# Branch A's attention scores as three products of rounded halves in place of one fp32 product, with another order of steps

## The reference, cut to what matters

```python
for layer in range(DEPTH):                      # DEPTH = 2
    u = rms_norm(h, norm_pre[layer])
    proj = u @ w_in[layer]                      # split into the columns of A, B, C, D
    y_a = mla_branch(...) * silu(a_g)
    y_b, y_c, y_d = ...                         # dilated, top-k sparse, differential attention
    y = concatenate([y_a, y_b, y_c, y_d]) @ w_out[layer]
    h = h + rms_norm(y, norm_post[layer])

# in mla_branch, for each block of 128 queries:
    s = (einsum('bqhd,bshd->bhqs', qn, k_nope) + einsum('bqhd,bsd->bhqs', qr, k_rope)) * scale
    s = where(keys <= t, s, NEG_INF)
    p = softmax(s);  out = einsum('bhqs,bshd->bqhd', p, v)
```

## Time and profile before

| | before |
|---|---|
| median of 3 runs | 665.01 us |
| lowest, highest | 664.68, 666.29 us |
| the profiled execution | 664.22 us, span 662.4 us |
| PE busy | 636.5 us, 96% of the span |
| DVE, ACT, POOL busy | 392.7, 355.8, 241.4 us (59%, 54%, 36%) |
| mean granted TensorE clock | 0.993 |

### The profile page before, as it was taken

The page is one execution under the profiler, slowest core; times in us unless marked ns, Lnnn a source line. Parts: engine busy times, 40 slices in busy tenths (PEclk is TensorE's granted clock), DMA queues, the critical chain, the costliest instruction groups (busy, mean ns, idle before and its releaser), DMA issues. The chain is left out here.

```text
span 662.4 us, 10348 instructions
## 1 busy us (share of the span) xinstructions
PE 636.5 (96%) x3700; PEld 521.5 (79%) x3700; DVE 392.7 (59%) x986; ACT 355.8 (54%) x818; POOL 241.4 (36%) x209
## 2 busy tenths in 40 slices
PE   6999999999999999999999999999999999999996
PEld 4977887777778767679998897777777876776996
DVE  4322775986868558640381249679787765764124
ACT  4522734585465586862353454456655648678121
POOL 1443343345043781023416433343424359300330
PEclk9999999998999999999999999999999999999999
DMA  8447967553452403212372587644535222130202
GB/s 261 127 138 227 269 206 230 194 160 89 97 140 72 139 1 116 76 28 101 98 223 64 171 261 228 173 137 118 169 84 128 77 82 79 64 128 1 96 33 96
DMA packets 78589, 85.78 MB, mean 129 GB/s; under 512 B 21013, under 2 KB 62229, under 8 KB 78537
## 3 DMA queue, kind: packets, MB, share of 16 engines
q1 hardware_dynamic: 78537, 85.11, 42.9%
HBM read 70.38 MB, written 13.94 MB: 127 GB/s over the span
## 5 line engine op out<-in xcount | busy, mean ns | idle before, releaser
L727 POOL TENSOR_TENSOR w_low<-w_raw,w_high 128x512 fp32r<-128x512 f32 (+2 forms) x156 | 198.9, 1306 | 346.2 <-ACT w_high L769 346.1
L1343 PE MATMUL bank<-uT,w_high 128*128 128x512 f32 x400 | 160.4, 401 | 1.7 <-DVE cqlow L1145 0.9
L1345 PE MATMUL bank<-uT,w_low 128*128 128x512 f32 x400 | 158.6, 397 | 0.0
L1344 PE MATMUL bank<-uT,w_high 128*128 128x512 f32 x400 | 158.3, 396 | 0.0
L882 ACT ACTIVATE probs<-probs,negmax 128x128 f32<-128x128 f32 (+3 forms) x160 | 88.7, 558 | 53.9 <-DVE negmax L1187 52.9
L769 ACT ACTIVATE w_high<-w_raw 128x1024 fp32r<-128x1024 f32 (+2 forms) x78 | 76.4, 1030 | 27.6 <-DMA w_raw<-in_w_out 24.3
L1343 PEld LDWEIGHTS bank<-uT,w_high 128*128 128x128 f32 x400 | 75.8, 189 | 19.6 <-issue 3.3
L1345 PEld LDWEIGHTS bank<-uT,w_low 128*128 128x128 f32 x400 | 75.4, 189 | 17.8
L1344 PEld LDWEIGHTS bank<-uT,w_high 128*128 128x128 f32 x400 | 75.6, 189 | 16.0
L1343 PE MATMUL bank<-w_high,mix 128*128 128x256 f32 x256 | 72.4, 283 | 0.0
L1344 PE MATMUL bank<-w_low,mix 128*128 128x256 f32 x256 | 71.8, 280 | 0.0
(11 more groups left out here) (167 smaller groups left out, 1016.8 us busy)
## 6 DMA issues: line engine op xcount, KB each, us to landing
w_raw<-in_w_in SPq DMA_DIRECT2D x27, 1024.0 KB, 5.4
w_raw<-in_w_out SPq DMA_DIRECT2D x8, 1024.0 KB, 4.8
parts_dram<-staging SPq DMA_DIRECT2D x12, 512.0 KB, 6.9
strips<-strips_dram SPq DMA_DIRECT2D x24, 256.0 KB, 4.9
dqk<-parts_dram SPq DMA_DIRECT2D x24, 256.0 KB, 4.2
hX<-in_x SPq DMA_DIRECT2D x8, 512.0 KB, 5.8
qidx<-parts_dram SPq DMA_DIRECT2D x12, 256.0 KB, 4.2
w_raw<-in_w_in SPq DMA_DIRECT2D x4, 512.0 KB, 5.7
```

The lines of the kernel that those rows point to most:

```text
L727: ins = nc.gpsimd.tensor_tensor(w_low[:, s, ks, 0:w], w_raw[:, s, ks, 0:w], w_high[:, s, ks, 0:w].bitcast(F32), ALU.subtract)
L1343: nc.tensor.matmul(out_ap, lh, rh, start=start, stop=False)
L1344: nc.tensor.matmul(out_ap, lh, rl, start=False, stop=False)
L1345: return nc.tensor.matmul(out_ap, ll, rh, start=False, stop=stop)
```

## The change

After branch A's queries and keys of two heads are written to `aqk`, ACT copies them to a rounded high part (`aqk_high`, in room `X`), and DVE subtracts that to get the low part (`aqk_low`, which takes the place of `aqk` in room `Y`). This is the new step `aside side pair`, with side 0 for queries and 1 for keys: four steps per layer, each 128 partitions by 1024 columns on ACT and on DVE. PE then computes each score block by the three fp32r products of `three`. As room `X` is now in use until branch A's last score, the load of `hX` moves from `norm 12` to `norm 15`.

```diff
+        aqk_low = at("aqk_low", "Y", [P, 2, HEADS, SEQ], F32R)
+        aqk_high = at("aqk_high", "X", [P, 2, HEADS, SEQ], F32R)
...
-                if step == ("norm", 12):
-                    sp.wait_ge(shifted, jobs_scored(l, 11))
+                if step == ("norm", 15):
+                    sp.wait_ge(shifted, jobs_scored(l, 15))
                     src = x[0] if l == 0 else h_dram
...
+                if kind == "aside":                                    # ACT
+                    side, pair = step[1:]
+                    act.wait_ge(scores_ready, l * NS + NS_IDX + S_AT[3 * HEADS])
+                    wait_unit_emptied(act, l * NU + UNIT_AT[("ak", pair) if side else ("aq", 2 * pair + 1)])
+                    if side:
+                        wait_unit_emptied(act, l * NU + UNIT_AT[("akr",)])
+                    hs = slice(2 * pair, 2 * pair + 2)
+                    nc.scalar.activation(aqk_high[:, side, hs, :], aqk[:, side, hs, :], ACT.Copy).then_inc(a_high, 1)
...
+                if kind == "aside":                                    # DVE
+                    dve.wait_ge(a_high, l * len(ASIDES) + ASIDES.index(step[1:]) + 1)
+                    nc.vector.tensor_tensor(aqk_low[:, side, hs, :], aqk[:, side, hs, :],
+                                            aqk_high[:, side, hs, :].bitcast(F32), ALU.subtract).then_inc(a_low, 1)
...
                     if br == "A" and step[2] == 0:                     # PE
-                        wait_unit_emptied(pe, l * NU + UNIT_AT[("ak", h // 2)])
-                        wait_unit_emptied(pe, l * NU + UNIT_AT[("aq", h)])
+                        last = max(ASIDES.index((side, h // 2)) for side in range(2))
+                        pe.wait_ge(a_low, l * len(ASIDES) + last + 1)
...
-                            ins = nc.tensor.matmul(b, aqk[:, 0, h, qs], aqk[:, 1, h, ks],
-                                                   start=True, stop=True)
+                            ins = three(b, aqk_high[:, 0, h, qs], aqk_low[:, 0, h, qs],
+                                        aqk_high[:, 1, h, ks], aqk_low[:, 1, h, ks], True, True)
```

The step list is written in another order throughout. One line of it, where the new steps stand:

```diff
-    scores 11 0 1, norm 10, ak 0, mix 7, spread 4, turn 9 3, turn 10 0, scores 11 1 4, pv 4, aq 1, aq 2, turn 10 1, turn 10 2
+    scores 11 0 1, ak 0, spread 4, mix 7, turn 9 3, norm 10, scores 11 1 4, turn 10 0, aq 1, pv 4, aside 1 0, aside 0 0, turn 10 1, aq 2, turn 10 2, turn 10 3
```

More of the change, by code:

```diff
@@ L117 @@
[L117 to L120, removed]
@@ L121 @@
-    scores 8 0 2, asplit, turn 6 1, turn 6 2, lead ga 0, turn 6 3, wide 3, turn 7 0, aroot, turn 7 1, wide 8, fill 9, spread 3, aload, scores 8 2 4, unit ga 0, fill 10, wide 9, turn 7 2, turn 7 3, akr
-    scores 9 0 1, fill 11, scores 9 1 4, pv 3
-    scores 10 0 1, aweights, lead ga 1, turn 8 0, turn 8 1, unit ga 1, mix 6, turn 8 2, spread 8, turn 8 3, turn 9 0, turn 9 1, spread 9, norm 8, scores 10 1 3, norm 9, turn 9 2, wide 4, scores 10 3 4, aq 0
-    scores 11 0 1, norm 10, ak 0, mix 7, spread 4, turn 9 3, turn 10 0, scores 11 1 4, pv 4, aq 1, aq 2, turn 10 1, turn 10 2
+    lead cq 0, unit cq 0, lead cq 1, unit cq 1, lead qi 0, unit qi 0, lead qi 1, unit qi 1, lead dq 0, unit dq 0, lead dq 1, idx 0, unit dq 1, idx 1, lead dv 0, lead dv 1, idx 2, unit dv 0, unit dv 1, idx 3, lead dv 2, idx 4, lead dv 3, idx 5, idx 6, unit dv 2, idx 7, topk 2, unit dv 3, lead dk 0, topk 1, unit dk 0, topk 2, lead dk 1, unit dk 1, topk 2, lead gd 0, unit gd 0, lead gd 1
@@ new lines @@
+    scores 0 0 2, topk 2, unit gd 1, scores 0 2 5, topk 1, lead gb 0, scores 0 5 7, unit gb 0, scores 0 7 8, lead gb 1, topk 1, norm 0, unit gb 1
+    scores 1 0 1, turn 0 0, turn 0 1, scores 1 1 4, lead ckv 0, topk 1, scores 1 4 7, topk 2, scores 1 7 8
+    scores 2 0 2, unit ckv 0, turn 0 2, topk 1, lead bq 0, turn 0 3, norm 1, unit bq 0, lead bq 1, turn 1 0, scores 2 2 3, turn 1 1, scores 2 3 8, topk 2, unit bq 1, turn 1 2, topk 1, turn 1 3, norm 2, squares_a, topk 2, lead bk 0, topk 1, unit bk 0, topk 1, lead bk 1, unit bk 1, pv 0, turn 2 0
@@ new lines @@
+    scores 3 0 3, turn 2 1, topk 1, dsum 0, scores 3 3 6, lead cqq 0, scores 3 6 8, norm 3, turn 2 2, wide 0, unit cqq 0, turn 2 3
+    scores 4 0 3, spread 0, turn 3 0, turn 3 1, topk 2, lead cqq 1, topk 2, turn 3 2, topk 1, unit cqq 1, turn 3 3, lead ck 0, scores 4 3 4
+    scores 5 0 2, pv 1, unit ck 0, turn 4 0, scores 5 2 4, topk 1, wide 1, norm 4, turn 4 1, dsum 1, topk 1, turn 4 2, norm 5, lead ck 1, unit ck 1, topk 1, lead bv 0, turn 4 3
+    scores 6 0 1, unit bv 0, turn 5 0, lead bv 1, wide 2, topk 4, unit bv 1, scores 6 1 4, turn 5 1, spread 1, topk 3, lead bv 2, topk 1, turn 5 2, topk 1, unit bv 2, lead bv 3, turn 5 3, topk 4, unit bv 3, asums, fill 8
@@ new lines @@
+    scores 7 0 1, lead gc 0, topk 1, unit gc 0, topk 1, scores 7 1 4, topk 1, spread 2, lead gc 1, topk 1, unit gc 1, turn 6 0, turn 6 1, norm 6, norm 7, pv 2
+    scores 8 0 2, asplit, turn 6 2, lead ga 0, turn 6 3, wide 3, turn 7 0, aroot, turn 7 1, fill 9, wide 8, fill 10, scores 8 2 4, aload, spread 3, unit ga 0, turn 7 2, turn 7 3, akr, fill 11, wide 9
+    scores 9 0 4, pv 3, lead ga 1, aweights, unit ga 1, turn 8 0, spread 8, turn 8 1, turn 8 2, norm 8, spread 9, turn 8 3, mix 6, turn 9 0
@@ L125 @@
+    scores 10 0 3, turn 9 1, norm 9, turn 9 2, wide 4, aq 0, scores 10 3 4
+    scores 11 0 1, ak 0, spread 4, mix 7, turn 9 3, norm 10, scores 11 1 4, turn 10 0, aq 1, pv 4, aside 1 0, aside 0 0, turn 10 1, aq 2, turn 10 2, turn 10 3
     scores 12 0 4, norm 11
-    scores 13 0 1, norm 12, turn 10 3, scores 13 1 2, aq 3, wide 5, turn 11 0, turn 11 1, scores 13 2 4, ak 1, turn 11 2, turn 11 3, mix 3, spread 5, mix 2, pv 5, turn 12 0, turn 12 1, av 0, turn 12 2
-    scores 14 0 2, turn 12 3, norm 13, turn 13 0, mix 4, av 1, wide 6, turn 13 1, scores 14 2 4
@@ L128 @@
-    scores 15 0 1, turn 13 2, spread 6, turn 13 3, norm 14, scores 15 1 4, turn 14 0, pv 6, turn 14 1, turn 14 2, turn 14 3, mix 5, turn 15 0, ya 0, norm 15, mix 0, turn 15 1, turn 15 2, wide 7, ya 2, turn 15 3, spread 7, pv 7, ya 1, mix 1
+    scores 13 0 2, wide 5, scores 13 2 4, turn 11 0, turn 11 1, ak 1, aq 3, turn 11 2, turn 11 3, mix 3, mix 2, spread 5, norm 12, aside 1 1, turn 12 0, pv 5, turn 12 1, aside 0 1, turn 12 2, av 0, norm 13
+    scores 14 0 2, turn 12 3, turn 13 0, mix 4, wide 6, av 1, turn 13 1, scores 14 2 4
@@ L129 @@
+    scores 15 0 1, turn 13 2, spread 6, turn 13 3, scores 15 1 4, pv 6, turn 14 0, turn 14 1, turn 14 2, mix 5, norm 14, turn 14 3, mix 0, turn 15 0, ya 0, norm 15, turn 15 1, wide 7, turn 15 2, ya 2, turn 15 3, ya 1, spread 7, pv 7, mix 1
 """
@@ L149 @@
 STEPS = layer_steps()
+ASIDES = [s[1:] for s in STEPS if s[0] == "aside"]
 WIDE_ORDER = [s[1] for s in STEPS if s[0] == "wide"]
@@ L1275, in _ @@
                     ins.then_inc(emptied_by["dve"], 1)
+                if kind == "aside":
+                    side, pair = step[1:]
+                    hs = slice(2 * pair, 2 * pair + 2)
+                    dve.wait_ge(a_high, l * len(ASIDES) + ASIDES.index(step[1:]) + 1)
+                    nc.vector.tensor_tensor(aqk_low[:, side, hs, :], aqk[:, side, hs, :],
+                                            aqk_high[:, side, hs, :].bitcast(F32), ALU.subtract).then_inc(a_low, 1)
                 if kind == "mix":
```

8 lines of the change are left out of this document (1 added, 7 removed).

## The result

The changed kernel takes 685.08 us (median of 4 runs, 682.34 to 686.22), beside 664.85 for the kernel before on the same chip (4 runs, 663.13 to 666.29). The ratio is 1.0306, with a 95% interval of 1.028 to 1.0331: slower by some 20 us, far outside the range that was forecast.

A forecast was written before the change was run, and what follows sets the result against it. PE, busy 96% of the span, was taken as the bound. Per layer -2.6 (order) + 0.4 (`spread 9`) + 1.5 (branch A) = -0.7 us, -1.4 for two, giving 663.3 us, range 659.0 to 667.8.

The forecast's parts named there:

- The other order: Branch D and behind it: reordered steps shorten PE's waits for score banks and DVE, 2.6 us less per layer.
- Two of the gains named: Head 1's wait for the mix of the maps, 0.3 us less; `turn 4 0` fills the wait behind `unit ck 0`, 0.5.
- The top-k rounds behind are late by that. I count nothing, because DVE is busy only 59%.: Branch D: top-k rounds delayed by DVE's stop at head 2 were costed at nothing.
- The standstill: DVE stands still some 2.5 us at head 2's first blocks, which overwrite probabilities that `turn 0 3` reads.
- The rival of the other side: Branch D's order gains nothing: DVE's lost 2.5 us delay the last top-k round and `fill 8`; 669 us, chance 0.15.
- `spread 9`: Ahead of branch A: it waits for a work bank DVE empties after the weight split; +0.4 us, between 0 and 1.5.
- Branch A: Its stage, per layer: waits for low parts +3.2, products -1.2, old waits swallowed -0.5, together +1.5 us.
- The 0.5 of old waits: Branch A's stage: of 2.4 us PE idle time, 0.5 per layer was taken to be swallowed by the new waits.
- The granted clock: Rival: one slow-clock window fewer gives 661.9 us, one or two more in the new waits 664.7 to 666.1; chance 0.12.
- The waits were not hidden: Answers a rival in which PE comes later and the low parts' waits are hidden; some 658.0 us, chance 0.16.
- No subtraction met POOL: Answers a rival in which three subtractions per layer meet POOL, each costing 1.7 us more; 673 us, chance 0.03.
- The two slower cases: Branch D's order giving nothing back (0.15) and a subtraction meeting POOL (0.03), which make up the chance of slower.

The follow-up runs named there:

- The front alone: Kernel before (fp32 scores) with the changed order of steps up to `asplit`, the order of before from there; ratio 1.0117, +7.8 us.
- front_rounds_later: Kernel before with the changed order up to `asplit`, but its old index part, and three top-k rounds moved later, behind `lead cqq 0`; ratio 1.0047.
- spread9_later: Changed kernel with the order of before up to `asplit`, and `spread 9` moved behind `turn 9 1`; ratio 1.0177, +11.8 us.
- the filling: Products adding nothing to the output, put into PE's waits: five places in the changed kernel (1.0194), two in the kernel before (0.9971).

## Why the prediction was wrong

**The other order (-2.6 per layer): the step that failed.** The front alone measured +3.9 per layer (7.8 for two). Two of the gains named are there: the waits for the mix of the maps fell from 0.9 to 0.4 us and those for `ckk` from 0.8 to 0.4, for both layers. Two costs outweigh them. The index part was not looked at, though a step moved in it; alone it costs 3.1 us in two layers. By the trace DVE's `select` starves while PE computes two half units, and PE then waits for it by way of ACT. And behind `pv 0`, where 0.7 was to be gained, the wait for head 3's blocks is what made the waits for branch D's blocks grow from 2.0 to 4.6 us in total.

**"The top-k rounds behind are late by that. I count nothing, because DVE is busy only 59%."** This is the sentence that was wrong. It dismisses a lag of DVE by a mean over the whole span, and in this stretch DVE works for 16.3 us without a pause: the low parts of `bk 1`, the gate of `pv 0` and head 3's blocks come late there, and PE waits for the last. front_rounds_later showed both that DVE's lag is the cause and that there is no free place near. The standstill itself was foreseen well (2.5 us, measured 2.83), but DVE had made up for it 12 us later. The lag that counts comes from a move that the prediction did not look at, `norm 2` behind `unit bq 1`, and 2.7 us of it from POOL. The rival of the other side had the right size of the standstill and the wrong end: it looked for the lag at `fill 8`, and no wait in PE's list is for that.

**`spread 9` (+0.4, bounds 0 and 1.5).** The mechanism was right: the wait for the gate behind the weight split is 2.0 us long. The stretch costs 1.6 per layer, four times the term and at its upper bound, with some 1.5 of doubt, and the halved clock behind it was not in the bound. But spread9_later showed that without this wait another one, of 1.48 us, takes its place.

**Branch A (+1.5 per layer).** It measured +4.8 (9.6 for two). The waits were well placed and sized: 1.86 and 1.44 us, 3.3, beside 3.2 in the prediction, though more than half of the first is a transpose that waits behind ACT's roundings, which the prediction had not queued there. The products gave 0.6 and not 1.2 (four heads at 2.16 less 2.02): 128 columns take 0.11 us (267.03 to 267.14), not 0.06, so the reckoning by columns fails for narrow blocks. The prediction had named the narrow block, but had taken off only 0.13 per head for it, where 0.29 was lost. The 0.5 of old waits that it let be swallowed did not show. The waits less the products make 2.7 of the 4.8; what is missing, 2.1, was not isolated. One halved stretch behind each first wait is the likeliest part of it.

**The granted clock (a rival with 0.12, one or two more stretches).** There were six more, each behind a new or longer wait; only the new waits ahead of head 14, 1.44 us, have none behind them. It was treated as an event beside the others, but it is a consequence of them: whoever forecasts a wait of PE of 1 to 3 us here must reckon with 0.9 to 1.7 us for the clock behind it (5.5 us for six by the filling, 10.4 by the clock rows).

**The other rivals.** The waits were not hidden. No subtraction met POOL: all eight took 1.20 to 1.23 us, as estimated. The mechanism of that rival was at work all the same, where the prediction did not look for it: it is `norm 2` that met POOL, 2.7 us per layer. The moved load cost nothing. The two slower cases add up to 0.18, where the prediction writes 0.17.

**The sum again.** For the two profiled executions, with spans 22.0 us apart: PE's waits grew by 12.1 us, the products gave 1.2, and the clock took 10.4 by its rows, 21.3 in all. By the filling it took 5.5, and then some 5.6 us are not accounted for. Which of the two is nearer was not settled.

## What to carry to other kernels

An engine's mean busy share says nothing of a stretch: where a change makes a helper engine late, list that engine's rows from there to its next real pause, and follow the first thing in them that the bounding engine needs. Where a step moves on DVE, look at what POOL does at its new place. Read the difference of the order on all stretches, also those far from the new work, since one step moved in the index part cost 3.1 us. And price a wait of PE with the clock behind it.

## What was not expected of the hardware

Short waits are enough to halve TensorE's clock. Behind waits of 1 to 3 us the granted clock fell to 1.2 GHz, and products whose result nobody reads, put into the same waits, kept it at 2.4 GHz and made three kernels faster: by 3.6, 7.4 and 1.9 us. Not every such wait is followed by a halved stretch (none stands behind the 1.44 us ahead of head 14), and the same program has more of them in one run than in another (0.995 to 0.985 in spread9_later); what decides this was not settled. The Trainium skill ("TensorE: Matmul & The Clock Gate", section "A second HAM failure mode: psum-queue depth-cycling") reports a kernel whose many short pauses between groups of matmuls made the clock go up and down, and that throughput was lost by it. By that, the trace agrees.
